# The first expert's rows by a product with a 0/1 matrix, leftovers behind its work, and another order of the first loads, in a two-layer float32 network on one core

## The reference

```python
def adaln(cvec, w_mod, b_mod):
    m = (jax.nn.silu(cvec) @ w_mod + b_mod)[..., None, :]
    return jnp.split(m, 6, axis=-1)
...
h = rmsnorm(x, norm_mix) * (1 + scale) + shift      # then h @ w_in
...
# every layer, tokens T = 512 (layer 0), 256 (layer 1), for each chosen expert e:
y_e = (silu(h[rows_e] @ w1[e]) * (h[rows_e] @ w3[e])) @ w2[e]
x = x + gate * sum_e weight_e * y_e
```

## Time and profile before

| | |
|---|---|
| median of 3 runs | 1248.27 us (1242.48 to 1249.26) |
| profiled execution | 1246.6 us, span 1245.0 us |
| PE busy | 1091.2 us (88%) |
| DVE, ACT, POOL busy | 504.4, 239.4, 229.2 us |
| moved by DMA | 311.40 MB, 250 GB/s over the span |
| mean granted clock of PE | 0.926 of full speed |

### The profile page before, as it was taken

One profiled execution on the slowest core, in us unless ns is written; L12 is line 12 of the kernel. 1 busy time (PEld: TensorE's weight loads), 2 busy tenths in 40 slices (PEclk: granted clock), 3 DMA queues, 4 the chain that ended last, 5 costly groups with the idle time before them and its releaser, 6 DMA issues.

```text
span 1245.0 us, 13497 instructions
## 1 busy us (share of the span) xinstructions
PE 1091.2 (88%) x5123; PEld 571.2 (46%) x5137; DVE 504.4 (41%) x941; ACT 239.4 (19%) x451; POOL 229.2 (18%) x234
## 2 busy tenths in 40 slices
PE   3899989798976999999994799998979489979997
PEld 1445455344443444444552554445643355534442
DVE  1345679452034222222225684327561543312214
ACT  2132132663023000000014331110110210100001
POOL 0201032000113433331203011000001254433000
PEclk8999989898987999999998899997569789999999
DMA  9732169604434799999998511240049459999993
GB/s 346 262 114 92 67 211 346 254 2 165 173 135 185 296 410 410 414 418 341 391 410 312 206 68 68 82 159 31 1 175 416 190 222 412 411 413 418 422 420 137
DMA packets 73213, 311.40 MB, mean 250 GB/s; under 512 B 10241, under 2 KB 12481, under 8 KB 55724
## 3 DMA queue, kind: packets, MB, share of 16 engines
q1 hardware_dynamic: 61915, 291.10, 59.8%
q0 software_dynamic: 10352, 16.00, 3.7%
q10 hardware_dynamic: 864, 3.15, 0.6%
HBM read 308.41 MB, written 16.65 MB: 261 GB/s over the span
## 4 chain that ended last, share of the span: by engine, by line
PE 72%; DMA 12%; DVE 7%; ACT 3%; issue 3%; SPq 1%; POOL 1%; ACTq 0%; DVEq 0%; POOLq 0%
DMA ring<-in_moe_w 10%; PE psum L2047 9%; PE psum L2044 9%; PE psum L1350 8%; PE psum L1255 7%; PE psum L618 6%; PE psum L2083 5%; PE psum L2078 5%; PE psum L610 3%; PE psum L416 2%; PE psum L1363 2%; PE psum L1631 2%; DMA ring<-in_w_mod 2%; PE psum L1630 2%; PE psum L554 1%
## 5 line engine op out<-in xcount | busy, mean ns | idle before, releaser
L2174 POOL DMA_INDIRECT arena<-hdram,idxl x128 | 128.7, 1005 | 270.7 <-DVE arena L2127 184.3
L2146 DVE TENSOR_TENSOR arena<-arena,psum 128x512 f32<-128x512 f32 x32 | 22.0, 687 | 279.6 <-PE psum L2044 149.4
L1350 PE MATMUL psum<-arena,ring 128*128 128x512 f32 (+1 forms) x256 | 97.8, 539 | 0.0
L1255 PE MATMUL psum<-ring,arena 128*128 128x512 f32 x192 | 82.9, 593 | 1.5 <-ACT arena L1240 1.5
L1279 POOL TENSOR_TENSOR wide<-wide,arena 128x512 f32<-128x512 f32 x12 | 15.2, 1268 | 346.3 <-DVE arena L1268 346.3
L2044 PE MATMUL psum<-arena 128*64 128x256 f32 x672 | 75.6, 381 | 2.2 <-DMA arena<-in_moe_w 1.1
L2044 PE MATMUL psum<-ring,arena 128*64 128x256 f32 x608 | 71.7, 393 | 5.4 <-DMA ring<-in_moe_w 3.7
L416 PE MATMUL psum<-ring,spad 128*32 128x512 f32 x384 | 57.0, 720 | 22.2 <-DMA ring<-in_w_mod 14.4
L2108 ACT ACTIVATE arena<-psum 128x512 f32<-128x512 f32 x32 | 19.1, 597 | 277.2 <-PE psum L2078 169.1
L2127 DVE STREAM_TRANSPOSE arena<-arena 128x1024 f32<-128x1024 f32 x32 | 64.9, 2029 | 16.5 <-DMA arena<-hdram,idxl 16.5
L2047 PE MATMUL psum<-arena 128*128 128x512 f32 x160 | 69.9, 593 | 1.6 <-DMA arena<-in_moe_w 1.6
(11 more groups left out here) (418 smaller groups left out, 1537.0 us busy)
## 6 DMA issues: line engine op xcount, KB each, us to landing
ring<-in_moe_w SPq DMA_DIRECT2D x46, 2048.0 KB, 13.9
arena<-in_moe_w SPq DMA_DIRECT2D x45, 2048.0 KB, 14.4
ring<-in_w_mod SPq DMA_DIRECT2D x24, 2048.0 KB, 8.4
ring<-in_od_w_in SPq DMA_DIRECT2D x6, 2048.0 KB, 11.2
wide<-in_moe_w SPq DMA_DIRECT2D x5, 2048.0 KB, 36.2
ring<-in_ev_w_in SPq DMA_DIRECT2D x3, 2048.0 KB, 21.4
arena<-ydram SPq DMA_DIRECT2D x6, 1024.0 KB, 8.1
ring<-in_ev_w_out SPq DMA_DIRECT2D x2, 2048.0 KB, 9.1
```

What stands on the lines that cost most here:

```text
L1255: mm = pe.matmul(bank(n % 6), catT[:, k, P * t:P * t + P], w[:, k, :], start=k == 0, stop=k == KD - 1)
L1350: mm = pe.matmul(bank(bk, tok.stop - tok.start), w[:, k, P * (b % 4):P * (b % 4) + P], hT[:, k, tok], start=k == 0, stop=k == KD - 1)
L2174: pool.indirect_dma_start(xq[e % NX][:, 256 * g:256 * g + 256], None, xrows(l), bass.IndirectOffsetOnAxis(ap=idxl[:, g, e:e + 1], axis=0), ...
```

## The change

Four things.

1. **Start.** The tokens are loaded right behind the constants. The order of mod chunks is 0, 2, 1, 3 (`FIRST_CHUNKS`), so that the shift and the scale of the first 512 features are known after two; the first projection's weights are loaded between chunk 2 and chunk 1. The norm is finished in halves, and `pe_first_projections` computes the first four `xbc` blocks in two half-sums, the lower halves among the rows of chunks 1 and 3.
2. **First expert.** DVE writes `hot`, a 0/1 matrix (128 tokens of a tile x 128 places) for expert 0, and `pe_first_gather` multiplies token rows with it into the transposed operand `xT[0]`, in two halves on two banks, which ACT copies. No DMA gather and no DVE transpose for expert 0. Expert e from 1 on is gathered as before.
3. **List products in bfloat16.** `lrow` and `listsum` are bfloat16.
4. **Leftovers behind it.** LIST0's rows stand in the router ahead of the positions. LIST1 (layer 1: `LIST_MOD1`) has its rows behind h(0) and its transposes behind at(0). y(0) follows at once. `pe_grow` and `pe_places` of layer 1 follow y(0). h(0) no longer waits for `rows_ready`.

```diff
-    FIRST = 4
+    FIRST_CHUNKS = (0, 2, 1, 3)
+    FIRST = len(FIRST_CHUNKS)
+    MODS = [(0, ch) for ch in FIRST_CHUNKS] + [(l, ch) for l in range(2) for ch in range(MODC) if l or ch >= FIRST]
...
-    before0 = [mod_src(*m) for m in MODS[:FIRST]]
-    before0 += [cols(ev, 512, 1024), cols(ev, 1024, EV_Q), cols(ev, EV_K, 2064), cols(ev, EV_Q, EV_K), cols(ev, 0, 512)]
+    before0 = [mod_src(*m) for m in MODS[:2]] + [cols(ev, 512, 1024)] + [mod_src(*m) for m in MODS[2:FIRST]]
+    before0 += [cols(ev, 1024, EV_Q), cols(ev, EV_K, 2064), cols(ev, EV_Q, EV_K), cols(ev, 0, 512)]
...
+    def pe_first_half(b, ks):
+
+        w = slot(2, 512)
+        for k in ks:
+            mm = pe.matmul(bank(b), w[:, k, P * b:P * b + P], hT[:, k, :], start=k == 0, stop=k == KD - 1)
+        if KD - 1 in ks:
+            mm.then_inc(S("in_full"), 1)
+
+    def pe_first_projections():
+
+        lower, upper_ = range(KD // 2), range(KD // 2, KD)
+        pe_first_norm(range(4, 7))
+        pe.wait_ge(*pe_more("ht_dve", 1))
+        weights_here(2)
+        for b in range(2):
+            pe_first_half(b, lower)
+        pe_mod_rows(2)
+        pe_first_half(2, lower)
+        pe_mod_cols(2)
+        pe_mod_rows(3)
+        pe_first_half(3, (0, 1))
+        pe_mod_cols(3)
+        pe_first_half(3, (2, 3))
+        pe_first_norm([7])
+        pe.wait_ge(*pe_more("ht_dve"))
+        pe.wait_ge(*pe_more("ht_act"))
+        for b in range(4):
+            if b == 0:
+                pe_first_half(b, (4, 5, 6))
+                pe.wait_ge(*pe_more("ht_dve"))
+                pe_first_half(b, (7,))
+            else:
+                pe_first_half(b, upper_)
...
-    lrow = view(3072, [6, P])[0:3 * E]
+    lrow = view(0, [3 * P]).bitcast(BF16).rearrange("p (g n) -> p g n", g=6)[0:3 * E]
+
+    hot = view(1024, [NT, P])
...
+    def pe_first_gather(tiles, half):
+
+        for k in range(4 * half, 4 * half + 4):
+            for i, t in enumerate(tiles):
+                mm = pe.matmul(psum[:, 4 + half, P * (k % 4):P * (k % 4) + P], htok[:, t, k:D:KD], hot[:, i, :],
+                               start=i == 0, stop=i == len(tiles) - 1)
+        mm.then_inc(S("pos_full"), 1)
...
+        if l == 0:
+            pe_mod_rows(LIST_MODS[0])
...
-        pe.wait_ge(*pe_more("slot1_ready"))
+        if l == 0:
+            pe_mod_cols(LIST_MODS[0])
+        pe.wait_ge(*pe_more("mask_ready"))
+        pe_first_gather(tiles, 0)
+        pe.wait_ge(S("slot1_ready"), 2 * l + 1)
...
+        pe_first_gather(tiles, 1)
...
+        act.wait_ge(S("pos_full"), 3 * l + 2)
+        act.activation(flat(xT[0][:, 0:4, :]), bank(4), ACT.Copy)
...
+        act.wait_ge(S("pos_full"), 3 * l + 3)
+        act.activation(flat(xT[0][:, 4:8, :]), bank(5), ACT.Copy).then_inc(S("xt_done"), 1)
...
+        place0 = rtv(652, [NT])[:, 0:n]
+        dve_step(dve.scalar_tensor_tensor(place0, pos[:, :, 0], 1.0, maskb[:, 0:n, 0], ALU.add, ALU.mult))
+        dve.scalar_tensor_tensor(hot[:, 0:n, :], bc(iotab.unsqueeze(1), n, P), 1.0, place0.unsqueeze(2).broadcast_to([P, n, P]),
+                                 ALU.add, ALU.is_equal).then_inc(S("mask_ready"), 1)
...
-        pe.wait_ge(S("rows_ready"), l + 1)
-        for e in range(E):
+        pe.wait_ge(S("slot1_ready"), 2 * l + 2)
+        both(pe_h, 0)
+        pe_mod_rows(LIST_MOD1 if l else LIST_MODS[1])
+        both(pe_at, 0)
+        pe_mod_cols(LIST_MOD1 if l else LIST_MODS[1])
+        both(pe_y, 0)
+        if l == 1:
+            pe_grow(1, 1, (0,))
+            pe_places()
+        for e in range(1, E):
             both(pe_h, e)
-            if e > 0:
+            if e > 1:
                 both(pe_y, e - 1)
             both(pe_at, e)
...
-        xt(0)
-        dve_mod(chunk)
-        if l == 1:
-            dve_mod_bias(1, 10, MODC)
-            dve_places()
-        xt(1)
...
+        if l == 1:
+            dve_places()
+        gate(0)
+        turned(0)
+        dve_mod(chunk)
+        if l == 1:
+            dve_mod_bias(1, 10, MODC)
+        xt(1)
+        y(0)
+        xt(2)
...
-        for e in range(2 + NX):
+        for e in range(1, 2 + NX):
+            if e == NX:
+                pool.wait_ge(S("idx_in"), 2 * l + 2)
             x(e)
...
-    used = [("mod_full", i + 1) for i in range(FIRST)]
-    used += [("in_full", n) for n in (4, 7, 11, 15, 19)]
+    used = [("mod_full", 1), ("mod_full", 2), ("in_full", 4), ("mod_full", 3), ("mod_full", 4)]
+    used += [("in_full", n) for n in (7, 11, 15, 19)]
...
+            for dst, src in TOKENS:
+                sp.dma_start(dst, src).then_inc(S("tokens_in"), 16)
...
-            if l == 0 and i == 1:
+            if l == 0 and i == 0:
                 for dst, src in PARAMS:
                     sp.dma_start(dst, src).then_inc(S("params"), 16)
-                for dst, src in TOKENS:
-                    sp.dma_start(dst, src).then_inc(S("tokens_in"), 16)
```

More of the change, by code:

```diff
@@ L450, in dve_mod_bias, with dve_first_bias, dve_first_acol @@
         dve.wait_ge(*dve_more("mod_done", 2))
-    ACOL_AFTER = {(0, 0): 2, (0, 1): 4, (1, 0): 6, (1, 1): 8}
+    ACOL_AFTER = {(0, 1): 6, (1, 0): 8, (1, 1): 10}
+    def dve_first_bias(j):
+        dve.wait_ge(S("mcol_done"), 2 * (j + 1))
+        v = mcol[:, 0, 0:4 * FIRST, :].rearrange("p (w i b) s -> p i w b s", w=2, i=2)[:, j]
+        v2 = bcol[:, :, 0:FIRST].rearrange("p b (w i) -> p i w b", w=2)[:, j]
+        for s_ in range(2):
+            dve_step(dve.tensor_tensor(v[:, :, :, s_], v[:, :, :, s_], v2, ALU.add))
+    def dve_first_acol(j):
+        ks = slice(4 * j, 4 * j + 4)
+        for s in range(2):
+            dve.scalar_tensor_tensor(acol[:, 0, 0, s, ks], mcol[:, 0, 8 + 4 * j:12 + 4 * j, s], 1.0, colsa[:, 4 * j:4 * j + 4],
+                                     ALU.add, ALU.mult).then_inc(S("acol_ready"), 1)
     def dve_acol(l, which):
@@ L499, in ht_bank @@
     def ht_bank(l, which, k):
-        return k % (7 if (l, which) == (0, 0) else 4)
+        return FIRST_BANK[k] if (l, which) == (0, 0) else k % 4
     def act_first_sums():
@@ L507, in act_first_sums, with act_first_rows, dve_first_rows @@
         act_rstd(NT)
-        act_mod(2)
+    FIRST_BANK = (4, 5, 6, 3, 4, 5, 6, 4)
+    def act_first_rows(j):
+        act.wait_ge(S("acol_ready"), 2 * j + 2)
+        for k in (4 * j, 4 * j + 2):
+            act_evac_ht(0, 0, ALL, k)
+        if j:
+            act_more("ht_full", 1)
+    def dve_first_rows(j):
+        dve.wait_ge(S("acol_ready"), 2 * j + 2)
+        for k in (4 * j + 1, 4 * j + 3):
+            dve_evac_ht(0, 0, ALL, k)
     def act_norm_rows(l, which, tiles):
@@ L546, in dve_norm_rows, with dve_evac_ht @@
         for k in range(1, KD, 2):
[L547 to L550, removed]
+            dve_evac_ht(l, which, tiles, k)
+    def dve_evac_ht(l, which, tiles, k):
+        dve.wait_ge(*dve_more("ht_full", 2))
+        for dst, src, a, b in ht_halves(l, which, tiles, k):
+            last = dve.tensor_scalar(dst, src, a, b, ALU.mult, ALU.add)
+        last.then_inc(S("ht_dve"), 1)
     def pe_norm_block(tiles, k, bk):
@@ L1221, in pe_grow @@
         blk = 16 + 24 * which
-        pe.wait_ge(S("mod_done"), (4, 8 + 4 * which)[l])
+        pe.wait_ge(S("mod_done"), (2, 6 + 4 * which)[l])
         pe.wait_ge(S("mcol_done"), ((NORM_MOD, COMB_MODS[0]), (NORM_MOD1, 2 * MODC))[l][which])
@@ L2014, in gathered @@
     def gathered(l, e):
-        in_layer = len(range(e % NX, E, NX))
-        return S(f"gathered{e % NX}"), 64 * (in_layer * l + e // NX + 1)
+        in_layer = len(range(e % NX or NX, E, NX))
+        return S(f"gathered{e % NX}"), 64 * (in_layer * l + e // NX + (e % NX > 0))
     def long_list(eng, l, e):
@@ L2113, in act_moe @@
                 act.wait_ge(S("at_full"), E * l + e - 1)
+            if e == 0:
+                act.wait_ge(S("hstored"), 16 * (NT + 2 if l else NT))
             act.activation(ah[e % 2], bank(hbank(e, 0)), ACT.Silu).then_inc(S("sil_done"), 1)
-            if e > 0:
+            if e == 0:
+                act_mod(LIST_MOD1 if l else LIST_MODS[1])
+                y(0)
+                if l == 1:
+                    act_grow((0,), [g_last])
+                    act_places()
+            if e > 1:
                 y(e - 1)
@@ L2134, in y, with gate @@
             dve.tensor_copy(yb[e % 2][:, 512:1024], bank(3)).then_inc(S("y_dve"), 1)
-        xt(0)
-        dve_mod(chunk)
-        if l == 1:
-            dve_mod_bias(1, 10, MODC)
-            dve_places()
-        xt(1)
-        for e in range(E):
+        def gate(e):
             b = e % 2
@@ L2153, in dve_moe @@
                 dve.wait_ge(S("y_full"), E * l + e - 1)
-            dve.tensor_copy(flat(aT[b]), bank(at_bank(l, e))).then_inc(S("at_done"), 1)
+            dve.tensor_copy(flat(aT[e % 2]), bank(at_bank(l, e))).then_inc(S("at_done"), 1)
+        if l == 1:
[3 more added lines that the diff above has]
+        dve_mod(chunk)
+        if l == 1:
+            dve_mod_bias(1, 10, MODC)
+        xt(1)
+        y(0)
```

(10 more changed lines are left out.)

98 lines of the change are left out of this document (48 added, 50 removed).

## The result

| | median | runs |
|---|---|---|
| before | 1248.27 us | 7 (1242.48 to 1251.29) |
| after | 1237.52 us | 7 (1236.86 to 1238.02) |

Ratio 0.9926 (95%: 0.9902 to 0.995): 0.7% faster, some 9 to 11 us of the 24.6 forecast. 1224 was predicted, and the range ended at 1236. The profiled execution took 1237.96 us, with a span of 1235.9 where before had 1245.0. In later sets of runs before's median was 1246.45 (17 runs), 1248.06 (11) and 1246.82 (11), and after's 1238.75 (6).

A forecast was written before the change was run, and what follows sets the result against it. First layer's MoE bound by PE (TensorE), the end by when weight loads run without a gap and how many remain. 6.8 + 8.5 + 9.3 = 24.6 off 1246.6 gives 1222.0; median 1.7 higher, say 1224 us; range 1213 to 1236.

The forecast's parts named there:

- The record of the product with the 0/1 matrix (0.12 us): Expert 0's product in both routers: each 128-column record, operand at a step of 8 floats, takes 0.12 us at full clock.
- a rival: 0.23 for 96 records, 10.6 us: Expert 0's product, both layers: strided operand costs 0.23 instead of 0.12 a record, 10.6 us lost, 1234; chance 0.1.
- near the only row: Reason for taking 0.12 between bounds 0.11 and 0.23: the only known strided f32 load, step 2, had records 0.12 apart.
- The start (6.8): Start to first four projection blocks: tokens loaded first, blocks done at 64.1 instead of 70.9, gain 6.8 us, range 5 to 8.5.
- The first layer (8.5): First layer's router and first expert: without gather, h of expert 2 starts 8.5 us sooner, range 5.7 to 9.
- The second layer (9.3): Second layer's MoE: ring slot free at 994.8, 40 loads left, stream of loads gains 9.3 us, range 6 to 11.
- Nothing for list products and constants: List products in bf16, beside the first expert's path, and 48 fewer constants: each predicted to gain nothing.
- the bound of a term: Start's low end: gain of 5 us instead of 6.8, with another 1.7 us at half clock.

The follow-up runs named there:

- E1: Changed kernel with expert 0's w1 and w3 loaded in another feature order, so the 0/1 product reads its stationary operand without a step: 1227.63 us.
- E6: Changed kernel with PE kept busy through the start by products never read, nine ahead of chunk 0's rows and fillers in gaps: 1235.65 us.
- E8: Changed kernel with both the operand without a step and the start's filler products, LIST_MOD1's rows left behind h(0): 1223.64 us.

## Why the prediction was wrong

**The record of the product with the 0/1 matrix (0.12 us)** is the step that failed first, and the most costly. It was carried over from a step of 2 to one of 8, where it measured 0.238. At 0.118 us too little for each of 96 records that is 11.3 us. The price was on record as a rival: 0.23 for 96 records, 10.6 us; E1 measured 9.9 to 11.1. What was wrong was its chance, 0.1, and the choice: "near the only row" was near in kind, but four times off in the size that mattered, and an unshown step belongs between its bounds, with both likely.

**The start (6.8)** gave 1.0 in the profiles, 2.7 to 3.9 in medians. The order of transfers and of work held: landings at 10.7, 16.4, 21.9, 27.3, 32.8 and 38.2 against 10.5, 16.1, 21.6, 27.0, 32.5 and 37.9. Wrong was the 2.0 us for 16 token transposes and the rows behind them at full clock, right after 12 us in which PE idled: the earlier trace rows had them at full clock behind two chunks of work that the change puts later. Left out were 1.1 us of waiting for DVE's copies of parameters. At full clock throughout E6 gains 6.2, near the forecast, but that is partly luck: it has chunk 0's rows at full clock too, for which the prediction allowed 1.7 us more (8.5).

**The first layer (8.5)** came to 0.3 from the norm to the MoE's end (291.2 to 290.9 us), and without the step to 8.2 (283.0). All its other terms held: rows ahead of the positions, h(0) at 13.97, leftovers behind it, no wait for a transfer.

**The second layer (9.3)** came to 6.1 from its norm to the end (278.2 to 272.1), and without the step to 8.2. The slot free at 994.31, a load sent right behind, 40 left: the mechanism was right. The time is near the forecast 994.8 only because after's second norm began 3.0 us sooner (963.82 against 966.82); counted from the norm the slot came free 30.5 us later, forecast 28.0. That is late by what the product took over its price (8.3 us for both halves, 3.8 to 6.8 priced). From the norm to the last load's landing it was 253.9 us before and 247.0 after.

**Nothing for list products and constants**: no run here contradicts it; it wasn't tried alone.

**The sum.** With the two wrong steps mended and all else as in the change (E8), the median is 1223.64, 23.2 below before's beside it, where 24.6 was forecast. So the accounting comes within 1.4 us of that once these two are mended, with E6's bit of luck in it. Each was priced by itself, as a rival or as the bound of a term: the range reached to one of them (1234) and ended at 1236; both together are 10.6 + 3 to 4, 1238.

## What to carry to other kernels

A float32 operand of TensorE that was read at a step of 3 floats or more cost 1.6 to 2.4 times a record at full clock. Make it contiguous by permuting the rows of the weight that it meets; that weight is loaded by DMA anyway, and its load, though somewhat longer, was off the path here. Price a moved stage at the clock that the traces show behind such work as now stands ahead of it, not at the clock of its old rows; behind 12.5 us of idle time PE ran at half. An edit that frees a slot earlier pays only if the next thing to free one follows within the transfers that it lets go.

## What the runs showed of the hardware that was not expected

- A 128x128 float32 record takes 0.112 to 0.118 us at step 1 or 2 and 0.22 to 0.24 at step 4 to 8, as stationary or moving operand; at half clock 0.213 for steps 1 to 3 and 0.240 for 8, so that the step's cost and the low clock's don't add.
- Step 12 is slower (0.267) than 8 (0.238), 16 (0.219) and 32 (0.220). No run tells why.
- Expert 0's w1 and w3, read in pieces of 2 KB a row instead of 16 KB a partition, took longer from issue to landing in E1 than in after: 8.4 and 11.1 us against 7.6 and 9.7 in the first layer, 16.9 and 9.8 against 15.4 and 7.4 in the second. They had landed 17 us or more ahead of h(0), which waited for ACT's copy and not for them.
- The view of stretches gives the granted clock as 1.00 from 16 to 24 in after, where chunk 0's rows take 3.64 us, the length at half clock: the trace has no record of the clock before its first change, at 29.3, and durations decide there.
